# Root on ScalarE, halves at the norms, and later convolution taps in a two-block transformer kernel

## The reference

```python
def rmsnorm(x, g):
    y = x * rsqrt(mean(x * x) + 1e-6)
    return y * g

# first block
h = rms_norm(x, pre_mix_norm)
proj = h @ w_in                      # q, k, v, u, v_s
attn = dilated_mixture_attention(q, k, v_a)
sgu = spatial_gating(u, v_s, ...)
y = concat([rms_norm(attn, ...), rms_norm(sgu, ...)]) @ w_out
x = x + rms_norm(y, post_mix_norm)
h = rms_norm(x, pre_ffn_norm)
f = (silu(h @ w_gate) * (h @ w_up)) @ w_down
x = x + rms_norm(f, post_ffn_norm)

# second block
h = rmsnorm(x, norm_mix)
proj = h @ w_in                      # q, k, v, z, xbc, dt, two gates
attn = windowed_gqa_sink(q, k, v, sink)
xbc = silu(depthwise_conv_centred(xbc, conv_w, conv_b))   # 5 taps over tokens
y = ssd_chunked forward + ssd_chunked backward + d_skip * xs
ssd = grouped_rmsnorm(y * silu(z)) * norm_g
merged = sigmoid(gate_a) * (attn @ w_a) + sigmoid(gate_b) * (ssd @ w_s)
x = x + merged @ w_out
x = x + cross_attention(rmsnorm(x, norm_cross), rmsnorm(mem, norm_mem))
x = x + square(relu(rmsnorm(x, norm_ffn) @ w_up)) @ w_down
return rmsnorm(x, norm_final)
```

## Time and profile before

| | us |
|---|---|
| median of three executions | 1997.96 (1993.83 to 2000.27) |
| the profiled execution, its own time | 2000.44 |
| its span | 1998.7 |
| TensorE busy / VectorE / ScalarE / GpSimd | 1880.9 / 1053.8 / 790.7 / 249.2 |
| mean granted clock of TensorE | 0.974 |
| weight hi on ACT (L760), weight lo on DVE (L1169), mean of 299 | 1.05, 1.24 |

### The profile page before, as it was taken

How to read it: one execution, slowest core, us unless ns; L and a number is a source line. 1 busy time by engine, 2 the same in 40 slices (tenths; PEclk the granted TensorE clock), 3 DMA queues, 4 the chain that set the end, 5 groups by cost and what they waited for, 6 DMA issues and landing times. The chain is left out here.

```text
span 1998.7 us, 24032 instructions
## 1 busy us (share of the span) xinstructions
PE 1880.9 (94%) x9382; PEld 1553.3 (78%) x9382; DVE 1053.8 (53%) x1802; ACT 790.7 (40%) x1486; POOL 249.2 (12%) x353
## 2 busy tenths in 40 slices
PE   6999899999998899888889889999999999999997
PEld 6777788888887777777777778777887888888886
DVE  5455443243345576786786764566555354343343
ACT  5255333231223355464553554445334333232231
POOL 1404100000001014123132141000020000000000
PEclk9999999999999799999999999999999999999999
DMA  6211233233233243342433334233433222232221
GB/s 223 74 54 55 76 116 101 90 95 113 87 95 100 74 128 107 95 124 88 131 112 116 116 106 179 74 106 106 148 123 126 79 75 95 84 117 95 84 85 63
DMA packets 127536, 205.64 MB, mean 103 GB/s; under 512 B 26288, under 2 KB 58224, under 8 KB 126784
## 3 DMA queue, kind: packets, MB, share of 16 engines
q1 hardware_dynamic: 118528, 169.19, 27.3%
q0 software_dynamic: 8320, 32.83, 4.8%
q10 hardware_dynamic: 576, 2.10, 0.3%
HBM read 191.37 MB, written 12.71 MB: 102 GB/s over the span
## 5 line engine op out<-in xcount | busy, mean ns | idle before, releaser
L1807 PE MATMUL m<-hH,hi 128*128 128x512 f32 (+1 forms) x1392 | 540.3, 388 | 8.9 <-DVE hL L1191 6.6
L1808 PE MATMUL m<-hL,hi 128*128 128x512 f32 (+1 forms) x1392 | 515.4, 370 | 0.0
L1809 PE MATMUL m<-hH,lo 128*128 128x512 f32 (+1 forms) x1392 | 515.2, 370 | 0.0
L1169 DVE TENSOR_TENSOR lo<-raw,hi 128x1024 fp32r<-128x1024 f32 x299 | 368.5, 1244 | 184.7 <-ACT hi L760 183.9
L760 ACT ACTIVATE hi<-raw 128x1024 fp32r<-128x1024 f32 x299 | 309.1, 1050 | 250.1 <-PE m L1820 139.4
L1807 PEld LDWEIGHTS m<-hH,hi 128*128 128x128 f32 x1392 | 268.0, 193 | 54.9 <-DVE hL L1191 7.1
L1809 PEld LDWEIGHTS m<-hH,lo 128*128 128x128 f32 x1392 | 267.3, 192 | 44.7
L1808 PEld LDWEIGHTS m<-hL,hi 128*128 128x128 f32 x1392 | 268.1, 193 | 40.8 <-issue 1.0
L1639 POOL TENSOR_SCALAR ST<-ST 128x1 f32<-128x1 f32 (+1 forms) x54 | 16.5, 306 | 1066.8 <-ACT junk L743 1066.5
L1818 PE MATMUL m<-hi,hH 128*128 128x512 f32 (+1 forms) x320 | 137.5, 430 | 0.0
L1820 PE MATMUL m<-hi,hL 128*128 128x512 f32 (+1 forms) x320 | 125.2, 391 | 0.0
(11 more groups left out here) (297 smaller groups left out, 2971.8 us busy)
## 6 DMA issues: line engine op xcount, KB each, us to landing
raw<-in_w_in_dram SPq DMA_DIRECT2D x72, 512.0 KB, 3.8
raw<-in_w_down_dram SPq DMA_DIRECT2D x54, 512.0 KB, 3.8
hn<-scr_cs_dram POOLq DMA_DIRECT2D x32, 512.0 KB, 4.3
raw<-in_w_up_dram SPq DMA_DIRECT2D x32, 512.0 KB, 4.5
raw<-in_w_gate_dram SPq DMA_DIRECT2D x44, 256.0 KB, 2.9
raw<-in_w_up_dram SPq DMA_DIRECT2D x44, 256.0 KB, 3.2
raw<-in_w_in_dram SPq DMA_DIRECT2D x33, 256.0 KB, 3.0
raw<-in_w_out_dram SPq DMA_DIRECT2D x16, 512.0 KB, 3.8
```

Of the source, the lines that this page charges most:

```text
L1169: e.tensor_tensor(d, r, h.bitcast(F32), ALU.subtract).then_inc(s_lo, 1)
L1807: e.matmul(bank, wh[:, kk, c], h[:, k, q], start=k == 0, stop=False)
L1808: e.matmul(bank, wh[:, kk, c], l[:, k, q], start=False, stop=False)
L1809: x = e.matmul(bank, wl[:, kk, c], h[:, k, q], start=False, stop=k == kt - 1)
```

## The change

**Norms.** ACT writes the squares of each half into an accumulator of its own. `mean_part` (Identity, scale 1/1024, bias EPS) turns that of the first half into its share of mean + eps, and `root` (Sqrt, scale 1/1024, bias that share) makes the root with the second half. DVE takes a reciprocal. POOL has no part in a norm but in 18 to 21, where it adds the halves and keeps the power. Four calls of `prepare_root` in slots (wo0 + 2, dn20 + 2, wa0 + 1, fd30 + 2) and one at the start run a Sqrt of one element.

**Boundaries.** For wo0 and wo1 ACT squares the bank itself, and DVE multiplies bank and gain into Y (the copy by ACT and `residual_gain` are gone). For dn20 and dn21 Y is squared and multiplied in halves. The residual add, hn, the final scale and the store of the output go in halves, and TensorE's transposes wait for the half they read. The slots of squares, hn and transposes move: at gu0 two earlier, at bc0 one, at wu1 the second stays, at xo the transposes are one later.

**Convolution and state space.** Two of the four taps stay in slot g and two go to g + 1; the steps behind them move by one slot (tanh, silu, transposes, the heads' last steps, OU). The first eight tiles' slots are spread more. On POOL PD and XW come ahead of the heads' DMAs and of OF, and the grouped norm's root comes last and a slot later.

**Prologue.** Gain 0 is loaded first, x tiles 0 and 1 first, then 2 and 3; weight units 1 and 2 wait for them; roundings come ahead of weight halves on ACT; constants, SBI, positions and WS load one unit later.

```diff
-    add("wo0", "tmt", 4, "aaaa")
-    add("wo1", "tmt", 4, "aaaa")
+    add("wo0", "tmt", 4, "dddd")
+    add("wo1", "tmt", 4, "dddd")
...
-for name in ("gu0", "bc0"):
+for name, late in (("gu0", 0), ("bc0", 1)):
     for t in range(4):
         base = s0(name) - 12 + 4 * t
-        N_SQ.append(base + 3), N_HN.append(base + 5), N_TR.extend([base + 6, base + 7 + (t == 3)])
+        N_S0.append(base + 1), N_S1.append(base + 2), N_HN.append(base + 3 + late), N_TR.extend([base + 4 + late, base + 5 + late])
...
-for base in (s0("wu1") + 4, s0("xo") + 6):
-    for t in range(4):
-        N_SQ.append(base + 4 * t), N_HN.append(base + 4 * t + 2), N_TR.extend([base + 4 * t + 3, base + 4 * t + 4])
+for t in range(4):
+    base = s0("wu1") + 4 + 4 * t
+    N_S0.append(FIN[BLK["wu0"].e0 + t] + 1), N_S1.append(base), N_HN.append(base + 1), N_TR.extend([base + 3, base + 4])
+for t in range(4):
+    base = s0("xo") + 6 + 4 * t
+    N_S0.append(base - 2), N_S1.append(base), N_HN.append(base + 2), N_TR.extend([base + 4, base + 5])
...
+ROOT_AT = (s0("wo0") + 2, s0("dn20") + 2, s0("wa0") + 1, s0("fd30") + 2)
...
-CV_T[:8] = [X0[0] + s for s in (-2, -2, 2, 3, 6, 9, 12, 16)]
-CV_AT, TH_AT, SL_AT = when(CV_T), when([s + 2 for s in CV_T]), when([s + 3 for s in CV_T])
-TN_T = [s + (7 if i % 8 < 2 else 5) for i, s in enumerate(CV_T)]
+CV_T[:8] = [X0[0] + s for s in (-2, -2, 3, 4, 8, 9, 13, 17)]
+CV_AT, TH_AT, SL_AT = when(CV_T), when([s + 3 for s in CV_T]), when([s + 4 for s in CV_T])
+TN_T = [s + (7 if i % 8 < 2 else 6) for i, s in enumerate(CV_T)]
 TN_T[1] += 2
+TN_T[5] += 1
...
-HD_AT = [when([s + d for s in HD_T]) for d in (-6, 0, 1, 2, 3, 5, 6)]
+HD_AT = [when([s + d for s in HD_T]) for d in (-6, 0, 1, 2, 3, 6, 7)]
...
-OU_T = [x + s for x in X0 for s in (44, 46, 60, 62)]
+OU_T = [x + s for x in X0 for s in (45, 47, 62, 64)]
...
+            def mean_part(c, done):
+
+                o.wait_ge(*done)
+                o.wait_ge(s_half, 2)
+                e.activation(st(c), st(c), ACT.Identity, bias=EPS[:, 0:1], scale=1.0 / D).then_inc(*o.own())
+
+            def root(c, done, sem, whole=False):
+
+                o.wait_ge(*done)
+                o.wait_ge(s_half, 2)
                 o.settle()
...
+                e.activation(st(c + 2), st(c + 1), ACT.Sqrt, bias=EPS[:, 0:1] if whole else st(c), scale=1.0 / D).then_inc(sem, 1)
...
+                if n in ("wo0", "wo1"):
+                    h, m = int(n[2]), i
+                    o.wait_ge(s_bank, b.e0 + i + 1)
+                    src = main[i][:, :]
...
+                done = square(src, st(ST_P[m] + h), s_psq)
+                if h:
+                    root(ST_P[m], done, s_prs)
+                else:
+                    mean_part(ST_P[m], done)
...
+                elif n[:2] == "wo":
+
+                    h = int(n[2])
+                    k = slice(512 * h, 512 * h + 512)
+                    o.wait_ge(s_psq, 4 * h + i + 1)
+                    o.wait_ge(s_gain[1], GAIN_LANDED[3])
+                    o.wait_ge(s_pv, 16)
+                    e.tensor_tensor(Y[:, i, k], bank[:, :], G[1][:, k], ALU.mult).then_inc(s_evd, 1)
...
+                for i in CV_AT.get(g - 1, ()):
+                    ct = conv_column(i)
+                    u, bank = CU[:, i % 2, :], main[i % 4]
...
+                for i in FN_AT[0].get(g - 1, ()):
+                    o.wait_ge(s_fsq, 4 * i + 4)
+                    rstd(st(ST_FIN[i], 4), 256, RMS_EPS, s_frs)
...
-                o.wait_ge(s_hn, n + 1)
+                o.wait_ge(s_hn, i + 1)
```

More of the change, by code:

```diff
@@ L239, in stat @@
     return _st[0] - n
-ST_N = [stat(1) for _ in range(22)]
-ST_P = [stat(1) for _ in range(8)]
+ST_N = [stat(3) for _ in range(22)]
+ST_P = [stat(3) for _ in range(8)]
 ST_AN = [stat(1) for _ in range(4)]
@@ L248 @@
 ST_X = [stat(12) for _ in range(4)]
-ST_OUT = [stat(1) for _ in range(4)]
+ST_OUT = [stat(3) for _ in range(4)]
 ST_A = [stat(8) for _ in range(32)]
@@ L365, in gains @@
 def gains():
-    before = [0, 5, 6, 26, 29, 36, 37, 104, 105, BLK["ws0"].u0, BLK["ws0"].u0 + 1, BLK["xq"].u0, BLK["up1"].u0]
+    before = [None, 5, 6, 26, 29, 36, 37, 104, 105, BLK["ws0"].u0, BLK["ws0"].u0 + 1, BLK["xq"].u0, BLK["up1"].u0]
     n, landed = [0, 0], []
@@ L736, in scalar_program, with square, prepare_root @@
             o = Order(e, o_act)
-            def square(x, acc, sem):
-                o.settle()
-                if square.last:
-                    o.wait_ge(*square.last)
-                e.activation(junk[:, 0:x.shape[1]], x, ACT.Square, accum_out=acc).then_inc(sem, 1)
-                square.count[id(sem)] = square.count.get(id(sem), 0) + 1
-                square.last = (sem, square.count[id(sem)])
-            square.last, square.count = None, {}
+            def square(x, acc, sem=None):
+                n = x.shape[1]
+                r = range(2) if n > 512 else (square.turn,)
+                for k in r:
+                    if square.last[k]:
+                        o.wait_ge(*square.last[k])
+                c = slice(0, n) if n > 512 else slice(512 * square.turn, 512 * square.turn + n)
+                square.turn = 1 - square.turn
+                y = e.activation(junk[:, c], x, ACT.Square, accum_out=acc)
+                if sem is None:
+                    y.then_inc(*o.own())
+                    done = (o.sem, o.n)
+                else:
+                    y.then_inc(sem, 1)
+                    square.count[id(sem)] = square.count.get(id(sem), 0) + 1
+                    done = (sem, square.count[id(sem)])
+                for k in r:
+                    square.last[k] = done
+                return done
+            square.last, square.count, square.turn = [None, None], {}, 0
+            def mean_part(c, done):
[5 more added lines that the diff above has]
+                o.wait_ge(s_half, 2)
+                o.settle()
+                e.activation(st(c + 2), st(c + 1), ACT.Sqrt, bias=EPS[:, 0:1] if whole else st(c), scale=1.0 / D).then_inc(sem, 1)
+            def prepare_root():
+                o.wait_ge(s_half, 2)
+                e.activation(junk[:, 0:1], EPS[:, 0:1], ACT.Sqrt).then_inc(*o.own())
+                square.last[0] = (o.sem, o.n)
             def split_weights(j):
@@ L1174, in norm_scale @@
                 i = 0 if n < 4 else 4 if n < 8 else 6 if n < 12 else 9 if n < 14 else 10 if n < 18 else 11
+                r = st(ST_N[n] + 2)
+                if n < 18:
+                    o.wait_ge(s_nrs, n + 1)
+                    e.reciprocal(r, r).then_inc(*o.own())
+                else:
+                    o.wait_ge(s_nrp, n - 17)
                 o.wait_ge(s_gain[i % 2], GAIN_LANDED[i])
-                o.wait_ge(s_nrs, n + 1)
                 if n >= 2:
@@ L1607, in vector_program @@
                     rest_products(b, i)
+                    if b.name in ("dn20", "dn21"):
+                        output_gain(b, i)
                 for m in P_AT.get(g - 1, ()):
-                    residual_gain(m)
-                for m in P_AT.get(g - 2, ()):
                     residual_add(m)
```

221 lines of the change are left out of this document (124 added, 97 removed).

## The result

The changed kernel took 1933.65 us in the median (1930.83 to 1935.68, four runs) against 1998.24 for the kernel before in the same series: a ratio of 0.968, 95% interval 0.966 to 0.970. I had forecast 1949 with a range of 1926 to 1982. The sign and the whole range held; the gain was 65 us where I had summed 51. The profiled execution took 1935.68, its span was 1933.9, the mean clock 0.99 (before 0.974).

What follows compares the result with a forecast made beforehand. TensorE's waits for VectorE's hn, POOL's XW and state-space products, with low clock behind them, were taken as the bound. Terms summed to 51.1 us: 2000.4 − 51.1 = 1949.3, range 1926 to 1982 (own range 1938 to 1962).

Steps and rivals of the forecast that it cites:

- State-space blocks: Four state-space blocks: four kinds of TensorE wait shrink, together 42 us, less a quarter: +32, bounds 15 and 50.
- (a): State-space blocks: PD and XW ahead of POOL's wait for squares; all XW waits and four slow stretches go, +19.9.
- (b): State-space blocks: waits for LOW, the gated norm's scale, go as its transposes move later: +5.1, and two slow stretches 3.4.
- (c): State-space blocks: OT ahead of the XW product comes sooner as two taps move away: +4.8, and one slow stretch 1.7.
- (d): State-space blocks: head waits fall some 5.8 a block, against a new 3.4 wait at z's bank 3: net +7.2.
- The quarter taken off for a full VectorE: State-space blocks: VectorE at 78% has full queues that make new waits, so 42 was cut to +32.
- First boundary: wo1 to gu0: shorter norm chain but earlier transposes; waits +1.9 and two slow stretches fewer +3.4, bounds 0 and 12.
- The rival that the norms gain nothing: Norms: in-order queues and not POOL set hn; only blocks, dt and tail count, 1964 us; chance 14%.
- Second boundary: dn21 to bc0: idle time 7.9 becomes 6.3, +1.6, and one slow stretch less, +1.7: +3.3, bounds 0 and 10.
- dt: dt steps: TensorE's 6.26 us wait for L1408 shrinks as four of eight taps move to later slots: +3, bounds 0 and 6.
- Third and fourth: Boundaries wu1 to xk and xo to up0: idle 3.8 to 1.4 and 3.6 to 0.8; +3.3 and +2.8, bounds 0 and 7.
- Prologue: Start of kernel: POOL's 0.74 leaves the chain, but weights wait for x: +0.4, bounds −3 and +2.

Runs made afterwards that it cites:

- the convolution's part: Kernel before with only two taps in slot g + 1 and the later slots of tanh, silu, transposes, heads and OU: 1964.61 us, ratio 0.9834.
- the pair of experiments: Kernel before with POOL's new order alone (1988.88 us) or the convolution's part alone (1964.61 us); with both, norms as before, 1947.62 us.
- the four other traces: Kernel before with POOL's new order (1988.88 us), the convolution's part (1964.61), both (1947.62), or one unused 4-byte tile ahead of hn (2006.54).
- the version with two loads per root: Changed kernel with a one-element Exp behind each of 20 norm roots, so tables load twice per root: 1973.37 us, ratio 0.9874.

## Why the prediction was right or wrong

**What bounds the kernel** was read rightly: the waits in the windows of the earlier trace rows are where most of the time came from, 53.5 of 65 in the state-space blocks. The sign and the order of the terms held; that 1934 stood within the range is in part luck, since the largest term was beyond its own bound and others took back 11 us.

**State-space blocks, +32 forecast, +53.5 measured,** beyond the bound of 50. Idle time gave 34.6 and the clock 18.7. Nearly all of the 34.6 shows by waits: XW 12.2, the head's two 10.4, LOW 5.1, OT ahead of XW 3.7, OT of the other line 5.0, less 2.1 for the tap. The terms were mis-sized in both directions.
- *(a) POOL's order.* The mechanism held: XW now stands ahead of the squares. Here is POOL in the changed kernel, to lay beside the earlier trace rows; the root is at 879.75, behind the PD and XW that it used to hold up:

```profile
875.31 0.78 POOL L1802 TENSOR_TENSOR PD<-PREV,CDEC 128x256 f32<-128x256 f32 x1 [2.33 <-ACT PREV L1088]
876.05 0.66 POOL L1807 TENSOR_TENSOR XW<-XS,WST 128x256 f32<-128x256 f32 x1
879.75 0.28 POOL L1739 TENSOR_SCALAR ST<-ST 128x4 f32<-128x4 f32 x1 [3.04 <-ACT junk L764]
```

  I gave it 19.9; alone it was worth 9.6, on top of the convolution's part 17.0. The step that failed was "and with it four slow stretches": alone it took away one. "Behind nothing" failed too when it stood alone: 3.6 us came back at the head's products.
- *(b) and (c) LOW and OT.* Rightly sized for the waits I named (LOW all of 5.1; OT 3.7 to 5.2 for 4.8), but the OT of the other line (7.5 to 2.6) was missing from the sum though the waits' view had it.
- *(d) The heads and z's bank.* The wait for the last tap came, at the place that I named, with 0.50 us and not 3.4:

```profile
831.84 0.75 DVE L1525 SCALAR_TENSOR_TENSOR X<-m,CST,X 128x510 f32<-128x510 f32 x1
832.65 0.50 PE L1913 MATMUL m<-hi,hH 128*128 128x512 f32 x1 [0.50 <-DVE X L1525]
```

  My step let TensorE come 2.1 us earlier against a tap that stayed where it was. But the tap waits for TensorE's last product of that bank, so it comes earlier as well; only the slot's delay counts against it. That was worth 3 × 2.9 = 8.7 us. The mean of 4.4 us a block for the head's waits was low as well: three blocks of before have 5.2 each and the first 1.8. In turn not all of them went; 7.0 of 17.4 us stayed.
- *The quarter taken off for a full VectorE* (10 us) had no mechanism, and nothing took it: VectorE is busy 81% of the blocks and TensorE idles 4%.
- *The clock.* I counted a stretch of 1.7 us per long wait, seven or so and part of three more; 11 of 12 went, 18.7 us. It can't be counted by the wait: the pair of experiments shows 1 and 6 for the parts and 12 for both.

**First boundary, +5.3, measured +9.8** (6.7 against the four other traces). I placed the waits at 0, 1.1, 3.3, 1.4 and 0.3; they are 0.23, 0.26, 2.37 and 1.00, idle time 3.9 for 8.0. The rest was again the clock, from 0.85 to 1.00; 3.1 of it is that execution's of before, which had 13.7 us at the lower level where the other four had 6.8. The term for a one-column Sqrt, 0.35 with bounds 0.2 and 0.6, is 0.295. The explanation by POOL (0.9 us of stretched power) was wrong in effect: with POOL back, nothing is lost (10.5 us over the same stretch). The rival that the norms gain nothing from POOL's release was right on that, and wrong that they gain nothing: what stayed when the roots went back (halves, the product from the bank, the earlier square) made the gain; which of the three was not told apart.

**Second boundary and dt** were right to 1 us (+3.9 for 3.3, +2.3 for 3). **Third and fourth** gave 3.4 for 6.1: at the third one wait of 2.4 and its slow stretch stayed, its clock is 0.96 as before. The fourth window is 3.2 us shorter, with 0.8 idle as I had said, but a wait of 1.48 for cross attention's oL is new at 1536.97, just ahead of it, and took half of that back.

**Prologue, +0.4, measured −3.7** in this execution, −1.7 to −5.0 in the six with this prologue; my bound was −3. I had named the cause (weights that land later behind x) and priced it as unlikely; the product at 18.64 came at 19.43, and the larger part is the wait at 37.60, which I had not followed to.

**Tail, +1, measured +3.7.** Chain and store gained 1.3, about what I said. The other 2.4 is POOL's own end of 6.8 us, which in the kernel before was 2.8 us later than the landing of the output at 1995.85; a view of waits doesn't show it.

**The feed-forwards, 0, measured −7.1.** The step was a term put at nothing: the sum took unedited products to cost the same, and no step looked at addresses. The errors of opposite sign, +21 in the blocks and −11 in feed-forwards and prologue, are why the sum came within 16 us.

**What hides the loads.** 15 table loads, as said, and none showed in TensorE's list of waits. The Trainium skill, "ScalarE: Activation LUTs", section *What ACT_TABLE_LOAD costs*, gives 2.66 us for each switch, 1.28 for the load and the rest a drain. This case's traces agree on the 1.28 and show no drain: in the version with two loads per root the load starts 0.02 us behind the instruction ahead of it, and the next one 0.01 behind the load.

```profile
235.60 0.19 ACT L765 ACTIVATION_READ_ACCUMULATOR junk<-X 128x1 f32 x1
235.80 1.28 ACT L790 ACT_TABLE_LOAD   x1
237.10 0.29 ACT L790 ACTIVATE ST<-ST 128x1 f32<-128x1 f32 x1
```

The same section of the Trainium skill has about 280 ns plus 0.83 per column for an instruction whose bias is a one-column pointer operand. By that page one column is 281 ns, an estimate; the rows have 294 to 295.

## What to carry to other kernels

In this kernel a stretch of low clock belonged to a neighbourhood of waits: price one edit by its waits alone, and expect the clock's part only when the last of the long waits near it has gone. When two engines are tied by a bank, move both in the sum. Before a difference of a few microseconds at one place is explained, look whether traces that leave the place alone agree on it. After any edit that adds or widens a small tile, compare the time of one unedited product in both traces: a shift of 32 bytes cost 8.6 us here, about what POOL's new order won by itself.

## What was not expected of the hardware

- A 512-column product whose stationary tile starts at 160, 192 or 0 modulo 256 bytes took 232 to 233 ns from start to start, at 128 it took 227; over this kernel 8.6 us from one unused tile of 4 bytes.
- In all six traces in which POOL works near the end, the program ended 6.8 us after POOL's last instruction: 1991.88 to 1998.7, and 1928.15 to 1934.9 with a memset of one element, 2.7 us of the metric.
- A one-column Identity or Sqrt with a one-column bias takes 0.295 us and the Sqrt without one 0.206, against 0.55 for POOL's power of one column. The engine that is faster at it was not the better place.
- In the blocks of the kernel before, 12 of the 18 gaps of 1.78 us and more stood ahead of a slow stretch of 3.4 us, while the 28 gaps of 0.28 to 1.03 us in the changed kernel's blocks stood ahead of none.
